# Two transformer blocks in float32 on one core: gates and branch products transposed, first loads on two queues, activation tiles at another start address

## Time and profile before

| | |
|---|---|
| median of three runs | 2849.26 us |
| the profiled execution, its own time | 2849.65 us |
| its span from first to last instruction | 2847.9 us |
| PE busy | 2822.8 us (99%) |
| DVE busy | 1815.2 us (64%) |
| ACT busy | 1450.6 us (51%) |
| POOL busy | 238.0 us (8%) |
| moved by DMA | 504 MB, 177 GB/s mean |
| mean granted clock of PE | 0.999 |

### The profile page before, as it was taken

The page is one execution under the profiler, slowest core; times in us unless marked ns, Lnnn a source line. Parts: engine busy times, 40 slices in busy tenths (PEclk is TensorE's granted clock), DMA queues, the critical chain, the costliest instruction groups (busy, mean ns, idle before and its releaser), DMA issues.

```text
span 2847.9 us, 44506 instructions
## 1 busy us (share of the span) xinstructions
PE 2822.8 (99%) x18116; PEld 2502.8 (88%) x18116; DVE 1815.2 (64%) x2700; ACT 1450.6 (51%) x2238; POOL 238.0 (8%) x187
## 2 busy tenths in 40 slices
PE   9999999999999999999999999999999999999998
PEld 8989879989989779989988887899799888878997
DVE  6646665646655676645468777665555687777655
ACT  5445555445445545444456555444344465655442
POOL 0010001010010011010013100010100131000100
PEclk9999999999999999999999999999999999999999
DMA  6544444545544445555555444555555454445553
GB/s 239 191 167 157 153 148 177 191 179 189 196 164 146 151 151 199 190 194 194 185 187 178 149 156 159 198 199 183 186 199 192 167 195 150 161 153 184 204 199 119
DMA packets 74779, 504.09 MB, mean 177 GB/s; under 512 B 8752, under 2 KB 10448, under 8 KB 18768
## 3 DMA queue, kind: packets, MB, share of 16 engines
q1 hardware_dynamic: 74576, 501.24, 49.2%
HBM read 500.12 MB, written 1.08 MB: 176 GB/s over the span
## 4 chain that ended last, share of the span: by engine, by line
PE 92%; DVE 4%; POOL 1%; ACT 1%; issue 1%; DMA 0%; SPq 0%; DVEq 0%; ACTq 0%
PE ps L1524 45%; PE ps L1542 39%; PE ps L1563 3%; POOL wlo L2452 1%; DVE conv L2281 1%; PE ps L1658 1%; DVE wlo L1987 1%; PE ps L1656 1%; PE ps L1683 1%; ACT whi L1728 0%; ACT conv L1898 0%; DVE ps L2098 0%; DVE stat L2103 0%; PE ps L1673 0%; PE ps L1674 0%
## 5 line engine op out<-in xcount | busy, mean ns | idle before, releaser
L1728 ACT ACTIVATE whi<-raw 128x1024 fp32r<-128x1024 f32 (+3 forms) x938 | 976.8, 1043 | 868.4 <-PE ps L1524 435.2
L1987 DVE TENSOR_TENSOR wlo<-raw,whi 128x1024 fp32r<-128x1024 f32 (+2 forms) x894 | 1080.6, 1220 | 301.9 <-ACT whi L1728 300.7
L1542 PE MATMUL ps<-xT_hi,whi 128*128 128x256 f32 x3296 | 927.3, 281 | 2.1 <-DVE wlo L1987 1.1
L1542 PE MATMUL ps<-xT_lo,whi 128*128 128x256 f32 x3296 | 920.5, 279 | 0.0
L1542 PE MATMUL ps<-xT_hi,wlo 128*128 128x256 f32 x3296 | 919.7, 279 | 0.0
L1542 PEld LDWEIGHTS ps<-xT_hi,whi 128*128 128x128 f32 x3296 | 619.4, 188 | 9.5 <-issue 6.9
L1542 PEld LDWEIGHTS ps<-xT_lo,whi 128*128 128x128 f32 x3296 | 619.7, 188 | 0.5
L1542 PEld LDWEIGHTS ps<-xT_hi,wlo 128*128 128x128 f32 x3296 | 619.4, 188 | 0.0
L1524 PE MATMUL ps<-whi,xT_hi 128*128 128x512 f32 (+2 forms) x1152 | 368.3, 401 | 1.5 <-DVE xT_lo L2006 0.8
L1524 PE MATMUL ps<-wlo,xT_hi 128*128 128x512 f32 (+2 forms) x1152 | 355.3, 389 | 0.2
L1524 PE MATMUL ps<-whi,xT_lo 128*128 128x512 f32 (+2 forms) x1152 | 355.1, 389 | 0.0
(11 more groups left out here) (316 smaller groups left out, 2365.5 us busy)
## 6 DMA issues: line engine op xcount, KB each, us to landing
raw<-in_w SPq DMA_DIRECT2D x436, 1024.0 KB, 4.8
vr<-in_vrows SPq DMA_DIRECT2D x19, 512.0 KB, 5.7
raw<-in_w SPq DMA_DIRECT2D x12, 768.0 KB, 4.2
raw<-in_w SPq DMA_DIRECT2D x10, 896.0 KB, 4.5
sums<-scratch SPq DMA_DIRECT2D x8, 512.0 KB, 4.5
raw<-in_w SPq DMA_DIRECT2D x4, 832.0 KB, 4.5
raw<-in_w SPq DMA_DIRECT2D x4, 576.0 KB, 3.7
x<-in_x SPq DMA_DIRECT2D x2, 512.0 KB, 6.4
```

The source lines that it names most:

```text
L1542: made = e.matmul(out, ws[:, o:o + 128], xs[:, kt, :], start=kt == 0 and n == 0 and c % 2 == 0, stop=kt == job.nk - 1 and n == 2, skip_gro ...
L1728: e.activation(out, raw, ACT.Copy).then_inc(*mark("hi", i))
L1987: e.tensor_tensor(out, raw, hi.bitcast(F32), sub).then_inc(*mark("lo", i))
```

## The change

1. `g1`, `g2` and both mixers' branch products go from `gemm` to `gemm_w`. Gate tiles become `[128, 24, 256]`, features on partitions. The second mixer's gate bias becomes a per-partition column (24 more columns per layer in `cols`), applied by ACT in the Sigmoid, two of 256 columns per bank straight from PSUM; the bias rows, DVE's bias add and the later Sigmoids of 1024 go.
2. `merge` works on two k-tiles of the transposed result; both sums are DVE's now, POOL has none. No transposes of the merged result: ACT and DVE split it into `xT` (`halve_o`, two k-tiles at a time) by a fiber per half, the first half's after the first piece of the last product, the second half's after the first piece of the output product.
3. The first mixer's order of branches is mla, dil, moba. The dilated input is transposed by a fiber during the first branch, into k-tiles 6 and 7 of `xT`. The pauses of the heads' fiber stop after its ninth step.
4. `columns` loops over the three products outermost and waits for the weights' low half only ahead of the third.
5. `ffn`'s chunk 0: both SiLUs go behind the chunk, at the background call after the next piece.
6. Start: `ident` and `cols` are issued by ACT's queue, `x` rows 0 to 127 come as two DMAs of 512 columns with a semaphore each, the third weight block as two DMAs with a semaphore each, and the first block's tables are issued during the first feed-forward.
7. Each Halves tile is preceded by padding, so that it starts at the same offset within 256 bytes as `whi` and `wlo`; `phalf` is allocated ahead of `xT`.

```diff
+LINE = 256
-BR1 = [(0, "w_br_mla", 3), (1, "w_br_moba", 3), (2, "w_br_dil", 2)]
+BR1 = [(0, "w_br_mla", 3), (2, "w_br_dil", 2), (1, "w_br_moba", 3)]
     def halves(name, nk, scope=ctx):
+        rest = (at_line - nc.sbuf_base) % LINE // 32 * 32
+        if rest:
+            scope.enter_context(nc.sbuf_tensor(name + "_rest", [128, rest // 4], F32))
...
     many("whi", NHL, [128, PIECE], F32R)
+    at_line = nc.sbuf_base % LINE
     many("wlo", NHL, [128, PIECE], F32R)
...
+        def first_chunk(c, h, h_free, banks, toks):
+            yield
+            for t in (0, 1):
+                silu(c, t, h, h_free, banks[t], toks[t])
             yield
             ps, free = self.aux.get()
             self.do("turn_h", s, c, h, ps, free, hT)
...
-                if s % 3 == 2:
+                if s % 3 == 2 and s < 9:
                     yield
...
-            toks = self.gemm(("g1", l, c), xt, 8, [[(b, 0, 512)] for b in banks], free)
+            tok = self.gemm_w(("g1", l, c), xt, 8, slices(banks), free)
...
+        def second():
+            yield
+            self.to_T([m["o_dil"][:, t, :] for t in (0, 1)], (("vec", "dil_o", l),), 2, oTd)
...
+        def merged(n):
+            for k in (4 * n, 4 * n + 2):
+                there = (xt.name, xt.gen, k)
+                self.do("halve_o", there, dst[:, k:k + 2, :], ("vec", "merged", key, l, k), xt, k, 2, xt.free)
+                xt.ready[k] = xt.ready[k + 1] = [("xlo", *there)] * 2
...
         for i, (r, nk) in enumerate(order):
+            last = i == len(order) - 1
             for n in (0, 1):
                 banks, free = self.two()
+                tok = self.gemm_w((key, l, r, n), ots[i], nk, slices(banks), free)
+                for k, b in zip((4 * n, 4 * n + 2), banks):
+                    self.do("merge", key, l, i, k, flat(dst[:, k:k + 2, :]), flat(G[:, 8 * r + k:8 * r + k + 2, :]), b,
+                            tok, gate[8 * r + k], plus, dst_free)
+                    self.main.put(b, ("merge", key, l, i, k))
+                if last:
+                    self.fibers.append(merged(n))
...
     def columns(i, job, lo_there, ready):
         pe.wait_ge(*at("hi", i))
-        pe.wait_ge(*at(*lo_there))
...
+        for n, (ws, xs) in enumerate(((hi, job.H), (hi, job.L), (lo, job.H))):
+            if n == 2:
+                pe.wait_ge(*at(*lo_there))
+            for j, (_, kt, _) in enumerate(kts):
+                for there in ready[j]:
+                    pe.wait_ge(*at(*there))
+                for c, out in enumerate(job.outs):
+                    o = j * w + 128 * c
                     made = e.matmul(out, ws[:, o:o + 128], xs[:, kt, :], start=kt == 0 and n == 0 and c % 2 == 0,
                                     stop=kt == job.nk - 1 and n == 2, skip_group_check=True)
...
+    def gate2(l, k, G, bank, tok, fence):
+        b = COLS[("gate_bias_2", l)] + k
+        act.wait_ge(*at(*tok))
+        act.wait_ge(*at(*fence[0]))
+        for j in (0, 1):
+            made = e.activation(G[:, k + j, :], bank[:, 256 * j:256 * j + 256], ACT.Sigmoid,
+                                bias=m["cols"][:, b + j:b + j + 1])
...
+        e.scalar_tensor_tensor(out=g if i else a, in0=g, scalar=plus, in1=bank[:, :], op0=add, op1=mul
+                               ).then_inc(*mark("merge", key, l, i, k))
+        if i:
+            dve.wait_ge(*at("merge", key, l, i, k))
+            if i == 2:
+                dve.wait_ge(*at("vec", "sum", key, l, k))
+            e.tensor_tensor(a, a, g, add).then_inc(*mark("vec", "merged" if i == 2 else "sum", key, l, k))
```

More of the change, by code:

```diff
@@ L328, in memory, with slices, flat, tiles_of @@
     return m
+def slices(banks):
+    return [b[:, 256 * n:256 * n + 256] for b in banks for n in (0, 1)]
+def flat(a):
+    return a.rearrange("p a b -> p (a b)")
+def tiles_of(a):
+    return flat(a[:, :, :]).rearrange("p (k x) -> p k x", k=8)
 class Order:
@@ L998, in mixer1 @@
             banks, free = self.two()
-            toks = self.gemm(("g1", l, c), xt, 8, [[(b, 0, 512)] for b in banks], free)
[L1000 to L1003, removed]
-        self.drain()
[L1005 to L1008, removed]
+            tok = self.gemm_w(("g1", l, c), xt, 8, slices(banks), free)
+            for k, b in zip((4 * c, 4 * c + 2), banks):
+                self.do("gate1", l, k, b, tok)
+                gate[k] = ("gate", "g1", l, k)
+                self.main.put(b, gate[k])
+        self.drain()
+        xt.free = (tok,)
+        oTd = Halves("oTd", xt.H[:, 6:8, :], xt.L[:, 6:8, :], 2)
+        oTd.gen, oTd.free = l, xt.free
+        def second():
+            yield
+            self.to_T([m["o_dil"][:, t, :] for t in (0, 1)], (("vec", "dil_o", l),), 2, oTd)
+        self.branches("br1", l, [(r, nk) for r, _, nk in BR1], [oTa, oTd, oTb], m["g1"], gate,
+                      tiles_of(m["xn"]), self.xn_free, second(), None, 1.0)
         self.product_out("o1", l, then, 0.5)
@@ L1016, in branches @@
             for n in (0, 1):
                 banks, free = self.two()
-                def merge(t, tok):
-                    a = dst[t][:, 512 * n:512 * n + 512]
-                    g = G[:, t, 1024 * r + 512 * n:1024 * r + 512 * n + 512]
-                    self.do("merge", key, l, i, n, t, a, g, banks[t], tok, gate[2 * r + n, t], plus, dst_free)
-                    self.main.put(banks[t], ("merge", key, l, i, n, t))
-                late = i == len(order) - 1 and n == 1
-                def mid(tok):
-                    merge(0, tok)
-                    for t in (0, 1):
-                        self.xn_free = (self.turn(dst[t], (("vec", "merged", key, l, 0, t),), t, 0, xt),)
@@ L1032, in branches @@
-                toks = self.gemm((key, l, r, n), ots[i], nk, [[(b, 0, 512)] for b in banks], free,
-                                 mid if late else None)
-                if not late:
-                    merge(0, toks[0])
-                merge(1, toks[1])
-            ots[i].free = (toks[1],)
+                tok = self.gemm_w((key, l, r, n), ots[i], nk, slices(banks), free)
[3 more added lines that the diff above has]
+                    self.main.put(b, ("merge", key, l, i, k))
@@ L1373, in build @@
         self.do("begin", 1)
[L1374 removed]
         enter = self.enter_scaled(0, self.col("ffn1_norm", 0, 8))
[L1376 removed]
+        first, other = enter(0, [("x0",), ("x0b",)], True)
         first()
@@ L2392, in stick @@
         e.tensor_tensor(z[:, :], z[:, :], w[:, 1:385], mul).then_inc(*mark("vec", "stick", l, h))
-    def gate2(l, c, t, g, bank, row, tok, there, fence):
-        dve.wait_ge(*at(*tok))
-        dve.wait_ge(*at(*there))
-        dve.wait_ge(*at(*fence[0]))
-        e.tensor_tensor(g, bank[:, :], row, add).then_inc(*mark("merge", "gate2", l, c, t))
     def tables2(fence):
```

142 lines of the change are left out of this document (52 added, 90 removed).

## The result

The changed kernel takes 2860.26 us (median of six runs, 2859.63 to 2860.52). Beside it the kernel before took 2849.62 us (2848.96 to 2850.41). The ratio is 1.0037, 95% interval 1.0026 to 1.0047: 10.6 us slower, where 2810 us, about 40 us faster, were forecast. The span of the profiled execution grew from 2847.9 to 2857.6 us. One execution of a kernel further down at a clock of 0.75 (3436.20 us, "The start alone") and one of the kernel before (7159.71 us) are in no ratio here.

A forecast was written before the change was run, and what follows sets the result against it. PE, busy 99%, was taken as the bound, its time the pace of the matmuls. From 2849.65 us, 11.3 came off without alignment and 29 with it, plus 0.5 for oT2: 2810 us, range 2790 to 2832 (chance 0.38).

The forecast's parts named there:

- Alignment: All long matmul streams: moving activation tiles to offset 0 speeds both forms; 29 us off, bounds 155 off to 47 more.
- Rival 3: Matmul streams: at equal offsets the two reads meet from their first address, every matmul loses; 2885 us, chance 0.18.
- Rival 1: Matmul streams: the offset doesn't matter, oT2's pace has another cause; 2840 us, chance 0.27.
- start: Kernel start: later SiLU, split loads and later tables let PE begin earlier and idle less; 2.3 us off, bounds 0 and 3.2.
- first mixers, with the clock: First mixers: 5.87 us of transposes and waits removed per layer, 3.5 new wait; 4.8 us off, plus 0.5 for the clock.
- second mixers: Second mixers: merged-result transposes removed, 1.85 us per layer, DVE's work hidden; 3.7 us off in all.
- rows to columns, oT2: Output-tile products in both layers: 384 matmuls lose oT2's faster rows pace, 4.3 ns each; 1.6 us more.
- feed-forward stages: Feed-forward: PE hardly waits for the later chunk 0 SiLUs past the start; 0 there.
- The clock: Second layer's long wait: shorter, so no drop to the lower clock expected; 0.5 us off, between 0 and 1.1.
- its gates: Second mixer's gate stage: ACT's 48 smaller Sigmoids, some 10 us more, stay hidden; 0, or 6 us in all if not.
- Dilated branch second: First mixer: its four transposes stay, about 4 us earlier, with the needed sum there; 0, heads' stage bounds -0.5 to +2.
- low half awaited later: Columns form: PE hardly waits for the weights' low half past the start; 0 there.

The follow-up runs named there:

- The start alone: Kernel before with only the change's first loads (two queues, halves), later tables and later chunk 0 SiLUs: 2847.45 us, ratio interval 0.9982 to 1.0002.
- stream-only kernel: Not a changed kernel: makes weight and activation pairs, then only streams TensorE at eight offsets, other engines idle; columns 119.9 to 120 ns at 0, 116.8 at 32.

## Why the prediction was wrong

**The step that failed** is the paragraph "Alignment". It had two columns matmuls and one rows matmul as one unit of 233.3 ns, moved 10130 such units together, and interpolated their pace at offset 0 from three places, of which the one that gave the slope, oT2, was of the rows form alone. At the offsets of before the two forms do cost the same (233.4 against 233.3), and I took that for a law. It is a coincidence of the offsets of before: already at 64 two columns matmuls take 235.6 ns, one rows matmul 233.1. The row that stood for "-64" was measured rightly: the stream-only kernel gives 228.8 ns at 192, against the 229.0 of the earlier trace rows, though this is one of two paces that rows have there (233.3 in the first block of the kernel at 192). And for rows matmuls even the direction was right: they went to 226.8 where the middle of my range was 230.4. But no row of before showed columns anywhere than at offset 32, and there the course is another: 119.9 at 0, 113.4 or 117.8 at 192. The side argument for a pace that falls on the way down from +64, 0.459 ns a column on cq against 0.455 on xT, was a difference of the product's width, not of its place: in the changed kernel both tiles lie at offset 0, and by the starts they take 133.2 / 288 = 0.463 and 174.0 / 384 = 0.453.

In the terms of the sum: rows matmuls that stayed rows gained 13.7 us on hT and 1728 x 5.3 ns = 9.1 on xT; columns matmuls that were columns already lost 29.7; the 1920 converted ones cost 3840 x 119.9 ns = 460.4 in place of 446.1, 14.3 more. Together +21.2, against the -28.5 forecast (the alignment with oT2's own half microsecond). That is the whole miss.

**Rival 3** had the sign right for the columns form and wrong for the rows form, and whether its mechanism (reads that meet at equal offsets) is the true one no run shows; its "from +0.9 ns on" could not be applied, since the unit fell apart. What I should have asked of it: is there any row that shows columns at a second offset? There was none, and so the bound upwards (+4.3 ns on the pair, a mirror) was a guess; a pair went up by 6.0.

**Rival 1**, "the offset doesn't matter", 2840 us, is what the kernel at offset 32 measures, 2840.03. It was worked out of the same rows as everything outside the alignment, so these terms were sound as a sum. That the sum fits within 0.2 us is in part luck, since the single terms are off by up to 3.7 us and cancel. One by one, by PE's starts with the stream pace taken out (us; each mixer is counted to the end of the long columns stretch that follows it; in brackets its two layers):

| step | forecast | measured | what the trace shows |
|---|---|---|---|
| start | -2.3 | -1.6 (-1.8 alone) | first columns matmul at 21.30 against 23.40 |
| first mixers, with the clock | -5.3 | -9.0 (-4.7, -4.3) | new wait 1.7 us a layer, not 3.5 |
| second mixers | -3.7 | -1.9 (-1.0, -0.9) | the 16 transposes went, a wait of 1.0 us a layer came |
| rows to columns, oT2 | +1.6 | in the streams | |
| feed-forward stages | 0 | +1.1 | stretches of a stream that do not keep its mean pace |
| sum without streams | -11.3 | -11.5 | |

*First mixer.* The timeline of PE at the end of the branches of the first layer, to be held against the earlier trace rows (start us, us, operands; the idle time ahead in brackets):

```profile
424.19 0.70 PE L1530 MATMUL ps<-whi,xT_hi 128*128 128x512 f32 x2 [1.31 <-DVE xT_lo L2107]
...
430.31 0.70 PE L1530 MATMUL ps<-whi,xT_hi 128*128 128x512 f32 x2 [0.43 <-DVE xT_lo L2107]
```

The wait is where the prediction put it, on DVE's split of the merged result, and of its size by the bounds (1.4 to 5.9). I took 3.5, nearer the upper end, because DVE was busy 20.80 of 20.90 us. A busy share of one only says that DVE had a queue, not how long it was; the 1.4 of "DVE enters without lag" was nearly right.

*The clock.* As predicted, with the shorter wait there is no drop in the second layer. How much of the 9.0 us this is cannot be told: the second layer, which had the drop, gained 4.3 us, the first 4.7. The same 4 us as in the earlier trace rows (busy per engine, granted clock, DMA share, GB/s):

```profile
1048.00:1052.00 4.00, 2.69 (x19) 2.34 (x19) 3.96 (x6) 2.94 (x4) 0.00 (x0) 1.00 0.53 193
```

*Second mixer, and its gates.* The transposes of the merged result are gone without a wait, 1.6 us of PE per layer by their starts. But the gates, which the prediction took at 0 as hidden, are not free. In each layer PE has a new wait of 1.0 us in the gate stage. The timelines there in the first layer, after and then before:

```profile
1739.96 1.91 PE L1570 MATMUL ps<-ident,ob 128*128 128x128 f32 x16
1741.14 1.55 ACT L1884 ACTIVATE g<-ps,cols 128x256 f32<-128x256 f32 x4
1742.57 3.04 ACT L1751 ACTIVATE oT_hi<-ps,cols 128x256 fp32r<-128x256 f32 x8
1743.45 3.23 DVE L2013 SCALAR_TENSOR_TENSOR oT_lo<-ps,cols,oT_hi 128x256 fp32r<-128x256 f32 x8 [3.14 <-ACT oT_hi L1751]
1746.04 0.49 PE L1663 MATMUL ps<-qkc 64*128 64x128 f32 x4 [0.98 <-DVE oT_lo L2013]
```
```profile
1738.62 1.91 PE L1563 MATMUL ps<-ident,ob 128*128 128x128 f32 x16
1739.88 3.00 ACT L1738 ACTIVATE oT_hi<-ps,cols 128x256 fp32r<-128x256 f32 x8
```

These are the transposes of the state-space branch's result. Before, ACT turned to their high halves 1.26 us after PE began them; now four Sigmoids of the gates stand ahead of them in its queue, and it is 2.61 us. DVE's low halves wait for ACT, and PE's next attention product waits for DVE. This is read from the timelines; no run takes the Sigmoids out of this place.

*Dilated branch second, low half awaited later.* The old loop order, with its earlier wait, gives the same time within 0.1 us. The dilated branch was not run by itself; the first mixers as a whole gained more than forecast.

The Trainium skill, TensorE: Matmul & The Clock Gate, section "Step-by-step: what each phase is for", says that loading the next weights takes no read bandwidth from the running matmul, the two having ports of their own. By this the offset should not matter. The runs speak against it as a rule for time: with every other engine idle, 256 columns take 113.4, 116.8 or 119.9 ns by nothing but the distance of the two operands' starts. That the two reads meet in the memory fits this; it was not shown.

## What to carry to other kernels

In these kernels, where TensorE streams float32r operands back to back, the distance between the start of the stationary and of the moving tile, modulo 256 bytes, was worth up to 6% of the matmul time (113.4 to 120.0 ns); measure it once for each form (which operand is stationary, how wide the moving one is) in a small kernel of streams alone, and only then choose addresses. Two forms that cost the same at one placement need not at another, so a change that moves tiles and converts matmuls must be priced as a table of form by placement. Expect a whole kernel to give less than the streams alone promise (33 us instead of 70 at 192), where a placement has two paces. And work out the addresses of an experiment before it runs: taking the padding out left the tiles where they were.

## What the runs showed of the hardware

Stretches of the stream-only kernels, each length over its count; ns for one rows matmul of 512 columns and one columns matmul of 256:

| offset | rows | columns |
|---|---|---|
| 0 | 226.9 to 227.3 | 119.9 |
| 32 | 233.1 | 116.8 |
| 64 | 233.1 | 117.8 |
| 96 | 234.4 | 120.0 |
| 128 | 232.1 | 120.0 |
| 160 | 233.3 | 117.3 |
| 176 | 230.2 | 119.2 |
| 192 | 228.8 to 229.4 (in the whole kernel also 233.3) | 113.3 to 113.6, or 117.8 |
| 208 | 231.7 | 119.2 |
| 224 | 233.3 | 118.3 |

The course is not smooth, and the best place for one form (0 for rows) is among the worst for the other. At 192 both forms have two paces; a stretch keeps the one that it has over hundreds of matmuls, and for columns interruptions of some kinds and counts change it. In the kernels before and changed, the first stream matmul behind a transpose or an attention product costs extra, about the same in both forms: by the medians for rows 318 ns (before) and 314 (changed) instead of 233 and 227, for columns 205 and 203 instead of 117 and 120, about 85 ns each. Directly behind another stream, of the other form or on another tile, the first matmul took its usual pace.
